# Two gathers of 4 KB rows in place of one of 8 KB rows in an expert-retrieval loop on one Trainium2 core

## What is computed

```python
def peer(h, w_query, sub_keys1, sub_keys2, expert_down, expert_up):
    ...
    def block_fn(xb):
        ...
        idx = jnp.take_along_axis(cand_idx, pos, axis=-1)
        g = jax.nn.softmax(top_s, axis=-1)
        u = expert_down[idx]
        act = jax.nn.gelu(jnp.einsum('thkd,td->thk', u, xb).astype(f32), approximate=False)
        return jnp.einsum('thk,thkd->td', (g * act).astype(xb.dtype), expert_up[idx])
```

## Time and profile before

| | |
|---|---|
| median of three runs | 4400.7 us |
| span of the profiled execution (first to last instruction) | 4384.4 us |
| median less span | 16.3 us |
| first gather of the loop starts at | 1435.3 us |
| first gather of the sample tokens starts at | 4341.9 us |
| 1024 gathers of 8 KB rows, mean on POOL | 1167 ns |
| 1024 dots on DVE, mean | 1227 ns |
| busy share of the DMA engines from 2000 to 4100 us | 0.95 |

### The profile page before, as it was taken

The page is one execution under the profiler, slowest core; times in us unless marked ns, Lnnn a source line. Parts: engine busy times, 40 slices in busy tenths (PEclk is TensorE's granted clock), DMA queues, the critical chain, the costliest instruction groups (busy, mean ns, idle before and its releaser), DMA issues.

```text
span 4384.4 us, 39661 instructions
## 1 busy us (share of the span) xinstructions
PE 3487.9 (80%) x11633; PEld 1922.7 (44%) x11633; DVE 2354.8 (54%) x4730; ACT 1050.6 (24%) x3019; POOL 1348.0 (31%) x1232
## 2 busy tenths in 40 slices
PE   7699996469997687786787788778769778877876
PEld 1698774135555342352353344335325324324432
DVE  0651111746663767457546646646755755664574
ACT  1110112123341222222222222222222222222222
POOL 0020110400000343344444443434444444443442
PEclk9799997689998898898899889889889889988988
DMA  7232210642323899999999999999999999999996
GB/s 273 69 103 110 82 61 31 246 165 86 101 72 134 345 374 374 381 384 366 361 389 368 376 375 379 366 370 380 382 384 378 381 374 383 377 375 375 395 382 272
DMA packets 210634, 1269.30 MB, mean 290 GB/s; under 512 B 25875, under 2 KB 51099, under 8 KB 74060
## 3 DMA queue, kind: packets, MB, share of 16 engines
q0 software_dynamic: 159504, 1114.68, 64.3%
q1 hardware_dynamic: 50902, 152.03, 9.9%
HBM read 1218.26 MB, written 48.36 MB: 289 GB/s over the span
## 4 chain that ended last, share of the span: by engine, by line
DMA 26%; PE 25%; issue 8%; ACT 4%; POOL 3%; DVE 3%; POOLq 0%; ACTq 0%; DVEq 0%; SPq 0%
DMA e_buf<-in_experts,e_idx 26%; PE ps L1771 22%; PE ps L1502 3%; POOL e_buf L1738 3%; DVE e_buf L1840 2%; ACT e_wts L1812 2%; ACT e_diag L1816 1%; ACT e_acts L1810 1%; DMA e_buf<-in_experts,e_idxT 0%; DMA r_wq<-in_w_query 0%; POOLq L58 0%; DVE r_work L1590 0%; DVE r_row L1591 0%; DVE r_work L1587 0%; DVE r_pos L1550 0%
## 5 line engine op out<-in xcount | busy, mean ns | idle before, releaser
L1771 PE MATMUL ps<-e_buf,e_diag 128*128 128x512 f32 x4096 | 2026.0, 652 | 638.7 <-ACT e_diag L1816 635.2
L1840 DVE SCALAR_TENSOR_TENSOR e_buf<-e_buf,e_h 128x1024 f32<-128x1024 f32 x1024 | 1248.2, 1227 | 1091.6 <-DMA e_buf<-in_experts,e_idx 1075.2
L1738 POOL DMA_INDIRECT e_buf<-in_experts,e_idx x1024 | 1195.4, 1167 | 1605.1 <-PE ps L1771 1406.3
L1771 PEld LDWEIGHTS ps<-e_buf,e_diag 128*128 128x128 f32 x4096 | 836.0, 210 | 1758.4 <-issue 990.9
L1810 ACT ACTIVATE e_acts<-e_dots 128x4 f32<-128x4 f32 x256 | 52.6, 205 | 2085.0 <-DVE e_buf L1840 2076.4
L1816 ACT ACTIVATE e_diag<-ident,e_wts 128x128 f32<-128x128 f32 x1024 | 327.3, 390 | 27.8 <-ACT e_wts L1812 2.7
L1502 PEld LDWEIGHTS ps<-r_h2T,r_wq 128*128 128x128 f32 x2304 | 269.3, 193 | 34.0 <-issue 34.0
L1502 PE MATMUL ps<-r_h2T,r_wq 128*128 128x128 f32 x2304 | 269.9, 276 | 3.1 <-DMA r_wq<-in_w_query 3.1
L830 PE MATMUL ps<-xo_w_out,xo_catT 128*128 128x512 f32 x512 | 224.5, 592 | 1.7 <-DVE xo_x L863 1.7
L1812 ACT ACTIVATE e_wts<-e_acts,e_gate 128x1 f32<-128x1 f32 x1024 | 218.5, 284 | 9.2 <-ACT e_acts L1810 1.1
L74 PE MATMUL ps<-p_wth,hT_high 128*128 128x512 f32 (+1 forms) x432 | 170.6, 395 | 10.9 <-PEq L413 10.9
(11 more groups left out here) (338 smaller groups left out, 3007.2 us busy)
## 6 DMA issues: line engine op xcount, KB each, us to landing
w_mod_sb<-in_w_mod SPq DMA_DIRECT2D x12, 2048.0 KB, 8.4
e_buf<-in_experts,e_idx POOLq DMA_INDIRECT x1024, 9.1
p_wt<-in_w_rows SPq DMA_DIRECT2D x6, 2048.0 KB
proj_d<-p_ev POOLq DMA_DIRECT2D x48, 256.0 KB, 2.3
x_zgv<-proj_d SPq DMA_DIRECT2D x8, 1536.0 KB
p_w<-in_w_chan SPq DMA_DIRECT2D x20, 512.0 KB, 4.3
r_wq<-in_w_query SPq DMA_DIRECT2D x4, 2048.0 KB, 20.2
xbc_d<-p_res POOLq DMA_DIRECT2D x12, 516.0 KB, 3.0
```

Source lines behind the costliest of these rows:

```text
L1738: return pool.indirect_dma_start(out=buf[s][:], out_offset=None, in_=io["experts"], in_offset=bass.IndirectOffsetOnAxis(ap=numbers, axis=0 ...
L1771: last = nc.tensor.matmul(g.bank(cols), diag[:, k % RING, :], buf[k % RING][:, D + cols * 512:D + (cols + 1) * 512], start=(k == 0), stop= ...
L1840: V.scalar_tensor_tensor(out=down, in0=down, scalar=1.0, in1=row, op0=ALU.mult, op1=ALU.mult, accum_out=out).then_inc(sem, 1)
```

## The change

The host no longer joins the two tables. Each slot has two gathers of 128 rows of 4 KB, 512 KB each: one into the ring `down0` to `down7`, one into the ring `up0` to `up7`. Both are issued by POOL, through the same queue. Eight down gathers are issued ahead of the loop. In slot k POOL waits until slot k - 8 is summed and issues the up gather of slot k; then it waits until slot k is dotted and issues the down gather of slot k + 8, across the tile's end where there is a next tile. The dots read `down`; they wait for `down_in`. The matmuls read `up`; PE has a second wait, on `up_in`, behind the one on `weighed`. The copy of the expert numbers now stands ahead of the down gather of slots 0 and 64. The memory taken and the instructions of DVE, ACT and PE are the same but for names and that wait.

```diff
-        buf = [sb(f"buf{s}", [P, 2 * D]) for s in range(RING)]
+        down, up = [sb(f"down{s}", [P, D]) for s in range(RING)], [sb(f"up{s}", [P, D]) for s in range(RING)]
...
-            def tile(n):
+            def gather(rows, table, numbers):
+                return pool.indirect_dma_start(out=rows[:], out_offset=None, in_=io[table],
+                                               in_offset=bass.IndirectOffsetOnAxis(ap=numbers, axis=0))
+
+            def take_down(n, k):
+                if k % HALF_SLOTS == 0:
+                    half = k // HALF_SLOTS
+                    ks = slice(half * HALF_SLOTS, (half + 1) * HALF_SLOTS)
+                    wait_apart(pool, rt.numbered, n * 2 + half + 1)
+                    nc.gpsimd.tensor_copy(idx[:, ks], rt.idx[:, ks]).then_inc(idx_kept, 1)
+                    wait_apart(pool, idx_kept, n * 2 + half + 1)
+                gather(down[k % RING], "down", idx[:, k:k + 1]).then_inc(down_in[k % RING], 16)
+
+            def tile(n, more):
                 for k in range(SLOTS):
                     wait_apart(pool, summed, n * SLOTS + k + 1)
-                    if k in (0, HALF_SLOTS - RING):
...
-                    gather(k % RING, idx[:, k:k + 1]).then_inc(landed[k % RING], 16)
-
-            with pool.Fori(0, NT) as n:
-                tile(n)
+                    gather(up[k % RING], "up", idx[:, k:k + 1]).then_inc(up_in[k % RING], 16)
+                    ahead = k + RING
+                    if ahead < SLOTS or more:
+                        wait_apart(pool, dotted, n * SLOTS + k + 1)
+                        take_down(n + ahead // SLOTS, ahead % SLOTS)
+
+            for k in range(RING):
+                take_down(0, k)
+            with pool.Fori(0, NT - 1) as n:
+                tile(n, True)
+            tile(NT - 1, False)
             pool.wait_ge(idxT_ready, 1)
+            wait_apart(pool, dotted, NT * SLOTS)
             for b in range(NS):
+                gather(down[b % RING], "down", idxT[:, b:b + 1]).then_inc(down_in[b % RING], 16)
                 wait_apart(pool, summed, NT * SLOTS + b + 1)
-                gather(b % RING, idxT[:, b:b + 1]).then_inc(landed[b % RING], 16)
+                gather(up[b % RING], "up", idxT[:, b:b + 1]).then_inc(up_in[b % RING], 16)
...
                     pe.wait_ge(weighed, n * SLOTS + k + 1)
+                    pe.wait_ge(up_in[k % RING], n * PER + 16 * (k // RING) + 16)
...
-                    dve.wait_ge(landed[k % RING], n * PER + 16 * (k // RING) + 16)
+                    dve.wait_ge(down_in[k % RING], n * PER + 16 * (k // RING) + 16)
...
-        "experts": np.concatenate([f["expert_down"][0], f["expert_up"][0]], axis=1),
+        "down": f["expert_down"][0], "up": f["expert_up"][0],
```

More of the change, by code:

```diff
@@ L1686, in experts @@
         h2_kept, idx_kept, generated = sem("h2_kept"), sem("idx_kept"), sem("generated")
-        landed = [sem(f"landed{s}") for s in range(RING)]
+        down_in, up_in = [sem(f"down_in{s}") for s in range(RING)], [sem(f"up_in{s}") for s in range(RING)]
         dotted, wch, weighed, summed = sem("dotted"), sem("wch"), sem("weighed"), sem("summed")
@@ L1736, in _ @@
         def _(pool):
-            def gather(s, numbers, **kw):
-                return pool.indirect_dma_start(out=buf[s][:], out_offset=None, in_=io["experts"],
-                                               in_offset=bass.IndirectOffsetOnAxis(ap=numbers, axis=0), **kw)
-            def tile(n):
+            def gather(rows, table, numbers):
+                return pool.indirect_dma_start(out=rows[:], out_offset=None, in_=io[table],
+                                               in_offset=bass.IndirectOffsetOnAxis(ap=numbers, axis=0))
@@ L1769, in tile @@
                     pe.wait_ge(weighed, n * SLOTS + k + 1)
+                    pe.wait_ge(up_in[k % RING], n * PER + 16 * (k // RING) + 16)
                     for cols in range(2):
                         last = nc.tensor.matmul(g.bank(cols), diag[:, k % RING, :],
-                                                buf[k % RING][:, D + cols * 512:D + (cols + 1) * 512],
+                                                up[k % RING][:, cols * 512:(cols + 1) * 512],
                                                 start=(k == 0), stop=(k == SLOTS - 1))
@@ L1787, in _ @@
                 pe.wait_ge(s_weighed, b + 1)
+                pe.wait_ge(up_in[b % RING], NT * PER + 16 * (b // RING + 1))
                 for cols in range(2):
                     last = nc.tensor.matmul(g.bank(cols, rows=NS), wpad[:, b, :],
-                                            buf[b % RING][:, D + cols * 512:D + (cols + 1) * 512],
+                                            up[b % RING][:, cols * 512:(cols + 1) * 512],
                                             start=(b == 0), stop=(b == NS - 1))
@@ L1838, in dot @@
             def dot(s, row, out, sem):
-                down = buf[s][:, 0:D]
-                V.scalar_tensor_tensor(out=down, in0=down, scalar=1.0, in1=row, op0=ALU.mult, op1=ALU.mult,
+                V.scalar_tensor_tensor(out=down[s][:], in0=down[s][:], scalar=1.0, in1=row, op0=ALU.mult, op1=ALU.mult,
                                        accum_out=out).then_inc(sem, 1)
@@ L1884, in _ @@
             for b in range(NS):
-                dve.wait_ge(landed[b % RING], NT * PER + 16 * (b // RING + 1))
+                dve.wait_ge(down_in[b % RING], NT * PER + 16 * (b // RING + 1))
                 dot(b % RING, spread(b), dots[:, b:b + 1], s_dotted)
```

## The result

The changed kernel takes 4367.6 us, the median of five runs (4355.99 to 4382.43); the kernel before took 4400.7 in the same comparison. The ratio is 0.9923, 95% interval 0.9899 to 0.9946. The forecast was 4525 us, 2.8% slower: the direction was wrong.

A forecast was written before the change was run, and what follows sets the result against it. The prediction took the ring's waits, close to the DMA engines' limit, as the bound before and POOL's issue after: 1435.3 + 1024 x 2.95 + 10 + 42.5 = 4508.6 us, plus 16.3: 4525 us, 2.8% slower; range 4230 to 4650.

The forecast's parts named there:

- With holds as frequent as now a slot costs POOL 2 x (1.167 + 0.30): POOL in the loop: two gathers at the old mean plus the gap before each, 2.93 us a slot.
- The price of a hold: POOL: a gather starting inside a dot waits for its end, then needs 0.82 us more; 0.55 us lost on average.
- first gather: Ahead of the loop: nothing changes, so the first prompt gather stays at 1435.3 us.
- a slot, us: The loop over 1024 slots: POOL's 2.93 us plus 0.02 for copies of expert numbers, 2.95 us.
- last prompt gather to first sample gather (starts): After the loop: with POOL the bound the queue is nearly empty, 10 us estimated between 0 and 23.8.
- from there to the span's end: From the first sample gather on: 16 gathers issue in about the time eight landings took; unchanged at 42.5 us.
- median less span of the profiled run: Outside the span: the median stood 16.3 us above the profiled run's span (4400.7 - 4384.4), added to the forecast.
- rival A: The loop: holds fall in step, two gathers to a dot, 2.65 us a slot, 4232 us (4140 to 4330); chance 0.27.
- lies near the upper end, where an always busy engine belongs: POOL in the loop: reason for taking 2.95 us a slot, near the 3.01 of dots met at random.
- PE's second wait: PE in the loop: one more semaphore per slot, put at nothing, at most 0.3 us without cover by idle time.
- The tile's end: Turn of tiles: DVE waits for the last sum; none of POOL's 4.81 us carried over, up to 34 us in range.
- the signs named ahead: Profile, if right: mean gather 1.1 to 1.25 us, DMA share 0.85 to 0.9, GB/s about 360; POOL's PE wait nearly gone.

The follow-up runs named there:

- e8: Changed kernel without the routing pieces of PE, ACT and DVE behind tile 0, whose expert numbers and gates serve all tiles: 4231.6 us, ratio 0.9658.
- e3: Changed kernel with gathers of 2 KB rows, 512 of the tables' 1024 columns, so half the bytes: 4535.4 us, ratio 1.0323.
- e1: Changed kernel with the token rows that the dots read held in PSUM in place of SBUF: 4128.0 us, 0.9392 of the kernel before.
- e4: Changed kernel without the lead, both gathers of a slot issued together when PE has freed it: 4461.8 us, ratio 1.0157.
- e6: Changed kernel without the lead, both gathers of a slot issued together, and the dots' token rows in PSUM: 4244.2 us, ratio 0.9668.

## Why the prediction was wrong

**The step that failed** is "With holds as frequent as now a slot costs POOL 2 x (1.167 + 0.30)". The price of a hold was right, its frequency was not. The mean gather is 1.086 us in place of 1.167: 24% are held, not 39%, for 0.58 us beyond an undisturbed one (0.57 before). The term measured 2.80 us a slot, not 2.95; over 1024 slots that is 158 us, and the whole span missed by 4508.6 - 4358.9 = 150. The other terms:

| term | predicted | measured |
|---|---|---|
| first gather | 1435.3 | 1441.0 |
| a slot, us | 2.95 | 2.80 |
| last prompt gather to first sample gather (starts) | 10 | 13.0 |
| from there to the span's end | 42.5 | 42.5 |
| median less span of the profiled run | 16.3 | 8.7 |

The last row was a slip of its own. The profiled run of the changed kernel took 4360.4 us, 1.5 more than its span; the other 7.2 are the distance of that run from the median. What I read as time outside the span was mostly such a distance, and a forecast for the median has no such term but the runs' spread. A smaller slip stands in rival A: 1504 + 1024 x 2.74 + 14 is 4324, not 4330.

The end, as in the earlier trace rows:

```profile
4303.38 0.95 POOL L1738 DMA_INDIRECT e_up<-in_up,e_idx  x1 [0.30 <-issue]
4316.34 0.94 POOL L1738 DMA_INDIRECT e_down<-in_down,e_idxT  x1 [12.02 <-DVE e_idxT L1882]
```

**Why the frequency changes.** I took it from a kernel in which POOL starts a gather when PE frees a buffer, at any point of a dot. Now POOL's own pace sets the starts, and dots follow the landings of what it issued. In the stretches of a tile without routing work on DVE that mostly falls in step, two gathers to a dot, as rival A had it (changed kernel, in order of time):

```profile
4284.63 0.95 POOL L1738 DMA_INDIRECT e_up<-in_up,e_idx  x1 [0.30 <-issue]
4284.65 1.23 DVE L1852 SCALAR_TENSOR_TENSOR e_down<-e_down,e_h 128x1024 f32<-128x1024 f32 x1 [1.26 <-DMA e_down<-in_down,e_idx]
...
4285.88 0.95 POOL L1738 DMA_INDIRECT e_down<-in_down,e_idx  x1 [0.30 <-issue]
...
4287.13 0.94 POOL L1738 DMA_INDIRECT e_up<-in_up,e_idx  x1 [0.30 <-issue]
4287.15 1.24 DVE L1852 SCALAR_TENSOR_TENSOR e_down<-e_down,e_h 128x1024 f32<-128x1024 f32 x1 [1.26 <-DMA e_down<-in_down,e_idx]
```

A dot begins 0.02 us after a gather's start, the second gather starts as it ends, and the pace is 2.50 us. Counted over the loop, 42% of the gathers that start inside a dot start in its last 0.13 us, where none is held; in the kernel before it is 14%, near the 11% that chance would give (0.13 of 1.23 us). Behind routing work, where DVE falls back and makes its dots in a row, it breaks (the same view; the first dot shown follows 6.8 us of routing on DVE and one dot more):

```profile
2722.68 1.22 DVE L1852 SCALAR_TENSOR_TENSOR e_down<-e_down,e_h 128x1024 f32<-128x1024 f32 x1
...
2723.83 1.22 DVE L1852 SCALAR_TENSOR_TENSOR e_down<-e_down,e_h 128x1024 f32<-128x1024 f32 x1
2723.88 1.99 POOL L1738 DMA_INDIRECT e_down<-in_down,e_idx  x1 [0.30 <-issue]
2724.97 1.22 DVE L1852 SCALAR_TENSOR_TENSOR e_down<-e_down,e_h 128x1024 f32<-128x1024 f32 x1
```

The gather that starts 0.05 us into a dot ends 0.82 us after it, as in the earlier trace rows. Grouped by stretch, a quiet one and one with routing work (count, busy us, mean ns, idle):

```profile
L1738 POOL DMA_INDIRECT e_up<-in_up,e_idx x24 | 24.7, 1030 | 7.3 <-issue 6.4 <-PE ps L1783 0.9
L1738 POOL DMA_INDIRECT e_down<-in_down,e_idx x25 | 23.6, 945 | 7.6 <-issue 6.7 <-PE ps L1783 0.9
...
L1738 POOL DMA_INDIRECT e_up<-in_up,e_idx x40 | 48.4, 1210 | 12.2 <-issue 7.6 <-PE ps L1783 4.6
L1738 POOL DMA_INDIRECT e_down<-in_down,e_idx x39 | 39.2, 1005 | 11.9 <-issue 11.3 <-PE ps L1783 0.6
```

The first is 2.58 us a slot, the second, 2.8. Over the six inner tiles, slots 8 to 31, ahead of the routing work on DVE, have 8% of their gathers held and 2.59 us a slot; slots 32 to 103, with it, 30% and 2.86 us; the first eight slots, behind the last tile's sum, 35% and 3.10 us. So rival A held in the quiet stretches, something like the forecast's 39% and 2.95 us came about at the turn of the tiles alone, and I had given each theory the whole loop. The argument "lies near the upper end, where an always busy engine belongs" was the weak one: it took an engine that never rests for one that meets dots at random. e8 shows that routing work is a part of it: without it 13.6% are held and 136 us go. It isn't all: one tile of e8 has over half of its up gathers held and another hardly any. That e8's 4231.6 meets the 4232 of rival A is luck, for that run is a mixture of both. e3 shows the other side: the same gathers with other landings keep 71% of the up gathers held, at 2.97 us a slot.

What puts the phase where it is, is open. Shorter landings went with more held gathers at three sizes of row, which shows no cause; a rule that gives the phase from the length of the loop (theory L) missed at 3 KB; and in e8 the phase differs between tiles of one execution.

**What was right.** POOL becomes the bound, its wait for PE goes, PE waits for the up half in place of the diagonals. A gather of 4 KB rows takes POOL the 0.94 us of 8 KB rows, and of 2 KB rows too (the 0.95 of e3), with the gap of 0.30. PE's second wait cost nothing that shows. The tile's end was at nothing and wasn't: eight slots take 24.8 us at a tile's start and 23.7 at its end, against some 21 in the quiet stretches, about 7 us a tile. Holds take 4.7 us of the eight slots at the start and 2.4 at the end, where the copy of expert numbers adds about one, against 0.7 in the quiet stretch; POOL does not stand there.

**What misled.** Among the signs named ahead, the DMA share (0.99) and the mean gather (1.086) pointed to A, the 379 GB/s between the two. The share could not tell: it counts packets that take longer while queues run short, 0.170 us on average here, and 0.16 in e1, which moved a tenth more.

The Trainium skill, "SBUF — State Buffer", section "Who interferes with whom", says that a DVE instruction with at most one SBUF input, outside the 2-port perf modes, does not contend with GpSimd. e1 agrees: one input moved to PSUM, and the mean gather fell from 1086 to 962 ns. The same section infers that a `tensor_tensor`, with both inputs in SBUF, doesn't stall a DMA issued by GpSimd, since descriptor generation needs the write interface alone. This case's gathers contradict it. At the end of each tile DVE has two `tensor_tensor` of one size in a row, line 1636 with one input in PSUM and line 1638 with both in SBUF (changed kernel, in order of time):

```profile
2177.85 1.22 DVE L1636 TENSOR_TENSOR f_y<-ps,f_gate 128x1024 f32<-128x1024 f32 x1 [10.51 <-PE ps L1783]
2178.57 0.95 POOL L1738 DMA_INDIRECT e_up<-in_up,e_idx  x1 [0.30 <-issue]
2179.11 1.22 DVE L1638 TENSOR_TENSOR f_x<-f_y,f_x 128x1024 f32<-128x1024 f32 x1
2179.82 1.33 POOL L1738 DMA_INDIRECT e_down<-in_down,e_idx  x1 [0.30 <-issue]
```

At each of the seven turns of tiles a gather starts in either: none is held by the first, and all seven by the second, to 0.82 us behind its end.

## What to carry to other kernels

Before an issue queue is given more instructions, price one on the issuing engine with what disturbs it, and remove the disturbance first: here one input of a dot moved to PSUM was worth 34 us before the change and 240 after it, and the two together make 4128 us, 6.1% below the kernel before. How often two engines collide is not a property that can be carried from one kernel to the next; here it was 24, 38 and 42% with POOL setting the pace each time. So price both the locked and the random case by stretch, and weigh them by the share of the loop that each holds. A DMA share near 1 is no proof of a DMA bound: 0.99 went with 379 GB/s here, and 1.02 with 416 in e1.

## What the runs showed of the hardware

Fewer bytes made a loop slower: 2 KB rows 4535 us, 3 KB 4528, 4 KB 4368, all with POOL full and undisturbed gathers of 0.95 us, but with 42, 38 and 24% of them held; without holds 2 KB rows took 4113.

A hold goes one way. The dots that run beside held gathers keep their length (1227 ns in both kernels, 1220 with one input in PSUM; in the kernel before the 505 dots in which a gather starts take 1228, the others 1225), and a dot that begins inside a gather delays neither (the quiet stretch above).

The granted clock of TensorE rose with the lead: 0.91 in the earlier trace rows, 0.99 in the same stretch after it, against 0.89 in e4 and 0.94 in e6 without lead. In the kernel before, PE stood up to 9.7 us at a time for a group's diagonals; with the lead it waits for landings, more often and more briefly (from 2000 to 4100 us 458 times for 408 us, up to 5.9). The mean matmul of the sums went from 652 to 617 ns; what that is worth was not measured apart.
